# MLP of a decoder step: products of 448 columns for 224 tokens, 64 tokens as stationary tiles

## What is computed

```python
def hybrid_layer(x, cache_k, cache_v, h0_re, h0_im, p):
    ...
    h = x + mix @ p['w_out']
    y = h + jnp.square(jax.nn.relu(rmsnorm(h, p['mlp_norm_g']) @ p['w_mlp_up'])) @ p['w_mlp_down']
```

## Time and profile before

| | us |
|---|---|
| median of three runs | 1184.19 (1182.78 to 1184.59) |
| the profiled execution's own time | 1184.51 |
| its span, first to last instruction | 1182.7 |
| TensorE (PE) busy | 1174.5 |
| DVE, ACT, POOL busy | 749.6, 425.8, 139.2 |
| HBM read and written | 185.8 and 5.3 MB |

### The profile page before, as it was taken

One profiled execution on the slowest core, in us unless ns is written; L12 is line 12 of the kernel. 1 busy time (PEld: TensorE's weight loads), 2 busy tenths in 40 slices (PEclk: granted clock), 3 DMA queues, 4 the chain that ended last, 5 costly groups with the idle time before them and its releaser, 6 DMA issues.

```text
span 1182.7 us, 20247 instructions
## 1 busy us (share of the span) xinstructions
PE 1174.5 (99%) x8492; PEld 1104.5 (93%) x8492; DVE 749.6 (63%) x754; ACT 425.8 (36%) x515; POOL 139.2 (12%) x83
## 2 busy tenths in 40 slices
PE   9999999999999999999999999999999999999998
PEld 7577576799999999999999999999999999999998
DVE  7899899899776565544555554555564455565454
ACT  6100012975544333333333433333433333433331
POOL 0322512000000000100000110000110000110000
PEclk9899999999999999999999999999999999999999
DMA  7453333534445444454545455554445554445553
GB/s 290 137 140 125 111 115 126 175 122 143 162 157 191 170 161 167 154 178 165 174 161 166 155 178 165 171 164 163 158 152 188 170 168 160 161 148 184 174 171 117
DMA packets 55192, 190.29 MB, mean 161 GB/s; under 512 B 7864, under 2 KB 10168, under 8 KB 54712
## 3 DMA queue, kind: packets, MB, share of 16 engines
q1 hardware_dynamic: 54824, 188.79, 47.9%
q10 hardware_dynamic: 288, 0.30, 0.1%
HBM read 185.82 MB, written 5.28 MB: 162 GB/s over the span
## 4 chain that ended last, share of the span: by engine, by line
PE 94%; DVE 3%; issue 1%; ACT 1%; DMA 0%; SPq 0%
PE psum L1367 94%; DVE states L745 1%; DVE states L933 1%; DVE out_turn L745 0%; DVE turn L745 0%; DVE out_turn L975 0%; PE psum L1486 0%; DMA w_raw<-in_w 0%; ACT gate L606 0%; DVE q_t L993 0%; ACT L531 0%; DVE q_t L745 0%; ACT au L554 0%; DVE carry_p L745 0%; DVE kv_t L1025 0%
## 5 line engine op out<-in xcount | busy, mean ns | idle before, releaser
L736 DVE TENSOR_TENSOR w_lo<-w_raw,w_hi 128x1024 fp32r<-128x1024 f32 x292 | 407.1, 1406 | 385.5 <-ACT w_hi L450 384.7
L1367 PE MATMUL psum<-mov_b,w_hi 128*128 128x288 f32 x2624 | 522.4, 295 | 0.3 <-ACT gate L606 0.3
L450 ACT ACTIVATE w_hi<-w_raw 128x1024 fp32r<-128x1024 f32 x292 | 306.2, 1057 | 481.5 <-PE psum L1367 480.7
L1367 PEld LDWEIGHTS psum<-mov_b,w_hi 128*128 128x128 f32 x2624 | 419.8, 188 | 1.6 <-issue 0.7
L1367 PE MATMUL psum<-mov_a,w_hi 128*128 128x288 f32 x2048 | 406.6, 295 | 0.0
L1367 PE MATMUL psum<-mov_b,w_lo 128*128 128x288 f32 x1312 | 385.4, 294 | 0.0
L1367 PEld LDWEIGHTS psum<-mov_a,w_hi 128*128 128x128 f32 x2048 | 327.7, 188 | 0.1
L1367 PE MATMUL psum<-mov_a,w_lo 128*128 128x288 f32 x1024 | 300.7, 294 | 0.0
L1367 PEld LDWEIGHTS psum<-mov_b,w_lo 128*128 128x128 f32 x1312 | 247.6, 189 | 0.0
L1367 PEld LDWEIGHTS psum<-mov_a,w_lo 128*128 128x128 f32 x1024 | 193.3, 189 | 0.0
L1367 PE MATMUL psum<-x_g,w_raw 128*128 128x288 f32 x640 | 163.9, 414 | 0.3 <-DMA w_raw<-in_w 0.3
(11 more groups left out here) (182 smaller groups left out, 520.3 us busy)
## 6 DMA issues: line engine op xcount, KB each, us to landing
w_raw<-in_w SPq DMA_DIRECT2D x335, 512.0 KB, 3.3
h_t<-in_x SPq DMA_DIRECT2D x3, 576.0 KB, 8.4
out_y<-h_t SPq DMA_DIRECT2D x3, 576.0 KB
b_w<-in_b SPq DMA_DIRECT2D x1, 1024.0 KB, 7.5
c_w<-in_c SPq DMA_DIRECT2D x1, 1024.0 KB, 7.3
k_cache<-in_kc SPq DMA_DIRECT2D x1, 1024.0 KB, 5.8
v_cache<-in_vc SPq DMA_DIRECT2D x1, 1024.0 KB, 7.0
out_kc<-in_kc SPq DMA_DIRECT2D x1, 992.0 KB
```

Source lines behind the costliest of these rows:

```text
L450: nc.scalar.activation(hi3[:, n % SLOTS, :], raw3[:, n % SLOTS, :], ACT.Copy) \
L736: nc.vector.tensor_tensor(lo3[:, n % SLOTS, :], raw3[:, n % SLOTS, :], hi3[:, n % SLOTS, :].bitcast(F32), ALU.subtract) \
L1367: return nc.tensor.matmul(out, lhs_t, rhs, start=start, stop=stop)
```

## The change

**Tokens in two parts.** A is the first 224 tokens, B the last 64. A tile of tokens is now stored as low A, high A, high B, low B (224, 224, 64 and 64 columns). Per output tile and `k` there are two products with a stationary weight tile (`streams`): `w_hi` passes over low A and high A together, 448 columns, into 448 columns of the bank; `w_lo` over high A and high B, 288 columns, into columns 224 to 511. At `k` = 0 the first has 512 columns (high B with it), so that all of the bank is begun anew.

**B stationary.** The product of `w_hi` with B goes the other way round (`passing`): the 128 columns high B and low B are the stationary tile, and `w_hi` of all the unit's output tiles passes, 384 or 256 columns, into a fourth bank. Its rows are tokens and have to be turned: at `k` = 0 the stationary tile is `first_b`, zeros and low B.

**Units.** A row (up or down) has six units of 3, 3, 3, 3, 2 and 2 output tiles, each with one bank a tile and one for B. The steps of the first four have 768 columns (384 KB), those of the last two 1024 with four `k` of 256. A row has 40 steps in place of 32.

**Turning back.** In an up row, ACT copies the B bank as its high part `bres_hi`, DVE takes the rest `bres_lo`, and TensorE multiplies both with `stack` (two unit matrices of 64 on top of each other) in f32r, 64 columns, into columns 448 to 511 of the unit's banks (`turn_b`). This stands in TensorE's program behind `k` = 1 of the next unit. In a down row DVE adds the B bank to `b_sum` in SBUF, and only the last row turns the sums, in fp32. DVE then adds the two parts of A in the banks (`low_sum`).

**States in halves.** `turn_h0` takes half of the pairs; the first half stands ahead of `u_t`, the second ahead of the second half's states, and the carry factors stand behind `u_t`. The first DMAs on SP change places: the first weights, then `small`.

```diff
-BLOCK_STEPS = 8 * GROUP_STEPS
+TOK_B = 64
+TOK_A = TOK - TOK_B
+UNIT_OUTS = (3, 3, 3, 3, 2, 2)
+ROW_UNITS = len(UNIT_OUTS)
+UNIT_STEPS = (8, 8, 8, 8, 4, 4)
+FIRST_OUT = tuple(sum(UNIT_OUTS[:i]) for i in range(ROW_UNITS))
+FIRST_STEP = tuple(sum(UNIT_STEPS[:i]) for i in range(ROW_UNITS))
+ROW_STEPS = sum(UNIT_STEPS)
+ROWS = 8
+BLOCK_STEPS = 2 * ROW_STEPS
...
+        bres_hi, _ = sb("bres_hi", 3 * P, F32R, at=at_t1)
+        bres_lo, _ = sb("bres_lo", 3 * P, F32R, at=at_t1 + 4 * 3 * P)
+        stack_r, _ = sb("stack_r", TOK_B, F32R, at=at_t1 + 4 * 6 * P)
+        b_sum, _ = sb("b_sum", KT * P, at=at_bw)
+        b_first, _ = sb("b_first", 2 * P, F32R)
...
+        HI, LO_A, LO_B = slice(TOK_A, TOK_A + TOK), slice(0, TOK_A), slice(TOK_A + TOK, 2 * TOK)
+        first_b = b_first[:, :].rearrange("p (x c) -> p x c", x=2)
+        HI_A, HI_B = slice(TOK_A, 2 * TOK_A), slice(2 * TOK_A, TOK_A + TOK)
...
+            sp.dma_start(raw4[:, 0, 0, :], ins["w"][0, :, 0:STEP_N]).then_inc(w_first, 16)
             sp.dma_start(small[:, 0:first], ins["small"][:, 0:first]).then_inc(small_loaded, 16)
-            sp.dma_start(raw4[:, 0, 0, :], ins["w"][0, :, 0:STEP_N]).then_inc(w_first, 16)
...
+            def act_up(row, past=0):
+                for u in range(ROW_UNITS):
+                    hi_ahead(u, row, past, SLOTS + 1 - UNIT_STEPS[u], SLOTS - 1)
+                    bres_from(u, row, past)
+                    hi_ahead(u, row, past, SLOTS - 1, SLOTS + 1)
+                    hid_his(u, row, past)
...
+            one_over_root(UNIT["rms_x"], r_b)
+            turn_h0(0)
...
+            turn_h0(1)
...
+            def low_sum(part, u, row, past):
+                nc.vector.tensor_copy(part[:, :, 0:TOK_A], mlp_outs(u, slice(0, TOK_A))).then_inc(low_copied, 1)
+                dve.wait_ge(low_copied, (2 * past + row) * ROW_UNITS + u + 1)
+                tt(part[:, :, 0:TOK_A], part[:, :, 0:TOK_A], mlp_outs(u, slice(TOK_A, 2 * TOK_A)), ALU.add)
+            def up_out(u, row, past=0):
+                lo_ahead(u, row, past, SLOTS + 1 - UNIT_STEPS[u], SLOTS - 1)
+                dve.wait_ge(bres_out, past * ROW_UNITS + row // 2 * ROW_UNITS + u + 1)
+                cols = slice(0, UNIT_OUTS[u] * P)
+                tt(bres_lo[:, cols], mlp_b(u), bres_hi[:, cols].bitcast(F32), ALU.subtract).then_inc(bres_split, 1)
+                if u >= 2:
+                    dve.wait_ge(hid_lo, past * ROW_UNITS + row // 2 * ROW_UNITS + u - 1)
+                lo_ahead(u, row, past, SLOTS - 1, SLOTS + 1)
+                part = sr4[:, u % 2, 0:UNIT_OUTS[u], :]
+                dve.wait_ge(b_turned, past * ROW_UNITS + row // 2 * ROW_UNITS + u + 1)
+                low_sum(part, u, row, past)
+                nc.vector.tensor_copy(part[:, :, TOK_A:TOK], mlp_outs(u, slice(2 * TOK_A, 512))) \
+                    .then_inc(mlp_free[(N_UNITS + u) % 2], 1)
+                own_freed(row, u, past)
+                nc.vector.scalar_tensor_tensor(part, part, 0.0, part, ALU.max, ALU.mult).then_inc(hid_ready, 1)
...
+                summed = tt(b_sum[:, cols], b_sum[:, cols], mlp_b(u), ALU.add)
+                if last:
+                    summed.then_inc(b_summed, 1)
+                lo_ahead(u, row, past, SLOTS, SLOTS + 1)
+                if last:
+                    dve.wait_ge(b_turned, N_BLOCKS * ROW_UNITS + u + 1)
...
                 dve.wait_ge(last_full, o + 1)
-                link(tt(tb4[:, 1, o, :], banks(N_UNITS + 3)[:, o, :], r_b[:, :], ALU.mult))
-                linked()
-                tt(h3[:, 12 + o, :], h3[:, 12 + o, :], tb4[:, 1, o, :], ALU.add).then_inc(last_ready, 1)
+                part, out = tb4[:, 1, o, :], psum[:, mlp_bank(u) + o, :]
+                link(nc.vector.tensor_copy(part[:, 0:TOK_A], out[:, 0:TOK_A]))
+                linked()
+                link(tt(part[:, 0:TOK_A], part[:, 0:TOK_A], out[:, TOK_A:2 * TOK_A], ALU.add))
+                link(tt(part[:, TOK_A:TOK], out[:, 2 * TOK_A:512], r_b[:, TOK_A:TOK], ALU.mult))
+                linked()
+                link(tt(part[:, 0:TOK_A], part[:, 0:TOK_A], r_b[:, 0:TOK_A], ALU.mult))
+                linked()
+                tt(h3[:, 14 + o, :], h3[:, 14 + o, :], part, ALU.add).then_inc(last_ready, 1)
...
+            def hid_los(u, past=0, before=0):
+                pool.wait_ge(hid_hi, past * ROW_UNITS + before + u + 1)
+                part, tiles = sr4[:, u % 2, 0:UNIT_OUTS[u], :], xb3[:, FIRST_OUT[u]:FIRST_OUT[u] + UNIT_OUTS[u], :]
+                tt(tiles[:, :, LO_A], part[:, :, 0:TOK_A], tiles[:, :, HI_A].bitcast(F32), ALU.subtract)
+                if u == 0:
+                    tt(first_b[:, 1, TOK_B:P], part[:, 0, TOK_A:TOK], tiles[:, 0, HI_B].bitcast(F32), ALU.subtract)
+                tt(tiles[:, :, LO_B], part[:, :, TOK_A:TOK], tiles[:, :, HI_B].bitcast(F32), ALU.subtract) \
+                    .then_inc(hid_lo, 1)
...
+            def streams(u, o, k, w, tile, turned=False):
+                slot, at, out = w
+                w_h, w_l = (t[:, slot, at + o * P:at + (o + 1) * P] for t in (hi3, lo3))
+                cols = 512 if k == 0 else 2 * TOK_A
+                mm(out[:, o, 0:cols], w_h, tile[:, 0:cols], start=k == 0, stop=False)
+                return mm(out[:, o, TOK_A:512], w_l, tile[:, HI], start=False, stop=k == KT - 1 and not turned)
...
+            def passing(row, u, k, w, tile):
+                slot, at, _ = w
+                return mm(mlp_b(u), tile[:, 2 * TOK_A:2 * TOK] if k else first_b[:, row % 2, :], hi3[:, slot, at:at + UNIT_OUTS[u] * P],
+                          start=k == 0, stop=k == KT - 1)
+            def turn_b(u, row):
+                if row % 2 == 0:
+                    pe.wait_ge(bres_split, row // 2 * ROW_UNITS + u + 1)
+                    parts = ((bres_hi, stack_r), (bres_lo, stack_r))
+                else:
+                    pe.wait_ge(b_summed, u + 1)
+                    parts = ((b_sum[:, FIRST_OUT[u] * P:(FIRST_OUT[u] + UNIT_OUTS[u]) * P], stack),)
+                for o in range(UNIT_OUTS[u]):
+                    for i, (src, unit) in enumerate(parts):
+                        done = mm(mlp_outs(u, slice(2 * TOK_A, 512))[:, o, :], src[:, o * P:(o + 1) * P], unit[:, :],
+                                  start=False, stop=i == len(parts) - 1)
+                done.then_inc(b_turned, 1)
...
+            def mlp_unit(row, u, between=None):
+                mov, per = (xa3, xb3)[row % 2], KT // UNIT_STEPS[u]
+                set_free(row, u)
...
+                for k in range(KT):
+                    w, tile = slot_of(u, row, k), mov[:, k, :]
+                    if row == 0 and u == 0:
+                        pe.wait_ge(h_lo, k + 1)
+                    if row % 2 == 1 and u == 0 and k in FIRST_OUT:
+                        pe.wait_ge(hid_lo, row // 2 * ROW_UNITS + FIRST_OUT.index(k) + 1)
+                    for o in range(UNIT_OUTS[u]):
+                        streams(u, o, k, w, tile, turned=row % 2 == 0 or row == ROWS - 1)
+                    done = passing(row, u, k, w, tile)
+                    if k % per == per - 1:
+                        done.then_inc(step_used, 1)
+                    if k == 1 and between:
+                        turn_b(*between)
```

385 lines of the change are left out of this document (221 added, 164 removed).

## The result

The changed kernel takes 1213.57 us (median of four runs, 1212.56 to 1220.65) where the kernel before takes 1184.13 us (1182.78 to 1184.59): a ratio of 1.0272 with a 95% interval of 1.025 to 1.0293 (the medians alone give 1.025). It is slower by 29 us. One of its four runs, that of 1220.65 us, had a mean granted clock of 0.948 where the others had 0.997 to 0.999. The prediction had said 1168 us, within 1157 to 1206, and gave slower a chance of 0.31: it was wrong in the sign and in the range. Of its rivals R2, that the time goes by columns (1205 us), was nearest; the result lies above that one too.

What follows compares the result with a forecast made beforehand. TensorE was taken as the bound, busy for 99% of the span. From 1184.5 us, -16.1 (MLP), +3.5 (waits), +0.9 (end) and -5.2 (states in halves) sum to -16.9, giving 1168 us, range 1157 to 1206.

Steps and rivals of the forecast that it cites:

- R2: Rival for the MLP: time goes by columns at 2.18 a ns, fewer products bring nothing; 1205 us, chance 0.13.
- The 12.2 ns: MLP: a 288-column product's 132.2 ns less 120.0 of columns, read as uncovered load and hand-over; wider products pay only 2.5 ns.
- (a): Start: ten f32r warm-up products at half rate show nothing over their columns, no charge per product or per column.
- (b): Full fp32 products and 128-column turns through the identity, full clock: some 2.5 ns each over their columns.
- (c): Every product loads its own stationary tile: 0.82 ns a column or 105 ns for 128, beside a fixed part.
- Turns: MLP: products that turn B's results back, taken at 109 ns each: 17.5 us, from 7 to 21.
- R4: Rival: the new order does not keep up in 12 large units, 1 us each, +12: 1180 us, chance 0.07.
- Waits of the last row: Last row: TensorE waits for the turns, 3 x 0.2 + 1.5 + 1.3 us, +3.5 us.
- Weights, DVE, ACT, POOL: MLP: weight loads in 320 steps in place of 256 and DVE's additional instructions stay hidden, at no cost.
- End: Behind the last product: five DVE instructions in place of two, +0.9 us.
- States in halves: Before the first u_t: wait falls to about 0.5 us (-1.9), clock stays full (-3.3); together -5.2 us (0 to -5.7).
- The first two DMAs: Start: their new order moves the start by under half a us; nothing taken.

Runs made afterwards that it cites:

- experiment 1: Kernel before plus a strip of f32r products of 64 to 512 columns behind its end: 230.0 ns for 512 columns, 203.3 for 448, 133.2 for 288, 118.7 for 256.
- experiment 2: Kernel before with 5944 of the MLP's 6144 products cut in two halves of 144 columns, same columns in all: 1717.06 us.
- experiment 5: Kernel before plus a strip: 192 columns f32r with 128, 64, 32 stationary columns 111, 89, 87 ns; f32r and bf16 in turns of 1 135.0 ns, of 16 127.7.
- experiment 7: Kernel after with the small tensor again sent for ahead of the first weights: 1210.91 us.
- experiment 6: Kernel before with only the states in halves, the order of the first two DMAs left: 1181.05 us against 1182.41, ratio 0.9988.

## Why the prediction was wrong, step by step

**The bound** was read rightly: TensorE was it and stayed it.

**The 12.2 ns** is the step that failed. The prediction read them as what a load of 128 columns and a hand-over lack to be covered by 120 ns of columns, and concluded that a wider product costs its columns and 2.5 ns. A floor by the load exists (experiments 1, 2 and 5), but at 111 to 112 ns, below 133. What stands above the columns is a surcharge of f32r products that grows from 12 ns at 256 columns to 17 at 512, of which 3.4 ns at 288 columns go by the load. So 448 columns cost 206 in place of 189 ns, +33 us; the sign of being wrong that the prediction had named, over 195 ns, came true. The three rows were read too far: (a), nothing over the columns at half rate, excluded a charge at half rate and said nothing of full rate, as the text itself remarked under R2; (b), fp32 with 2.5 ns over, moves its bytes at half the rate; (c) gave 105 ns for a load, and the 27 ns to 132 were given to a hand-over that no row shows. The turns of (b), at 109 ns with loads of 128 columns, had already shown such a load through in less than 132, as the prediction said against itself. That the 256-column products would cost 132 ns was wrong with it: 118.

**R2** had the right side and nearly the seven-product time (1190). Its proportion is too simple, as experiment 1 shows, but its price for 448 columns (205.7 ns) is what the MLP showed. That is partly luck: the strip has 203.3, and a law by columns alone gives 118 at 256 and 235 at 512 for the 118.7 and 230.0 measured. It was given 0.13, though nothing but (b) spoke against it.

**Turns**: 17.5 us forecast, 16.2 measured, and nobody waited for them in the up rows. Right, and R4 was wrong. The f32r turns of 64 columns went at 111 ns, so the 109 that were taken from wider fp32 turns stood close to the floor.

**Waits of the last row**: +3.5 forecast. Measured are two places, before the two small units, in which the next product starts 1.58 and 2.14 us after the one before where 0.12 is usual, so 3.5 us in all. The split was off: 1.5 and 1.3 there and three times 0.2 before, of which nothing came. The clock was at its lower level for 3.4 us behind the second (about 1.7 us more), which was not forecast. Undoing both gave 4.5 to 5.3 us.

**Weights, DVE, ACT, POOL**: hidden, right (DMA share 0.52, DVE busy 515 of 842 us), but for one wait of 0.6 us for w_lo in the first up row, which the forecast had without waits.

**End**: +0.9 us forecast, 0.86 measured in DVE's instructions.

**States in halves**: the gap fell by 1.8 us and the clock stayed, as forecast, and yet the 1.9 us were not gained: the first group ended 2.3 us later, and TensorE resumed 0.5 us later than before. **The first two DMAs** were valued at nothing and cost some 1.9 us (experiment 7). The clock's fall was counted with 3.3 us as if it were in each run; it cost 2.5 us in the trace that the forecast was reckoned from, and of six traces with this front three have none there (experiment 6). Together the start brought 1.6 us at the MLP (265.48 in place of 267.12 us), not 5.2, and against the trace of before in which the clock never fell (264.46) it brought nothing.

The sum: the MLP took 42 us more than forecast and the start gained 3.6 us less, and 1168 becomes 1213.

## What to carry to other kernels

Before products are made wider to save a charge per product, measure one width that the kernel doesn't have yet: strips of 60 products behind its end tell charge, slope and floor apart in one run (here to within 3 or 4 ns of what the same product took in the kernel). Where products are bound by their columns, look at the type of the operands, not at the number of products, and keep products of one type together: 4096 bf16 products shortened the MLP by 3.6 us scattered and by 27.6 us in order. A second order of DMAs at the start deserves its own run, since it decided here when the first products start and how many of them run at the lower clock. And look at more than one trace before a fall of the clock is put into a sum: one trace shows it as if it were always there.

## What the runs showed that was not expected

- f32r at full clock costs 7.4 ns and 0.435 ns a column from 256 to 512 columns, bf16 its columns at 2.4 a ns and 2.5 ns; moving data at a distance of eight bytes cost two cycles a column in either type.
- The load of 128 stationary f32r columns is a floor of 111 to 112 ns, and of 213 ns at the lower clock; for bf16 56 ns a product was reached.
- Changing between f32r and bf16 costs some 14 ns for a pair of changes in turns of up to 4.
- The clock fell to its lower level in stretches in which TensorE was busy all the time: in products of 64 columns, and in four of six traces behind attention's products of 128 and 16 columns near 262 us; but not in 1333 us of products of 144 columns (experiment 2). Behind the gap ahead of u_t it fell in three of six traces, and not by the length of the gap alone (1.65 us did, 1.81 didn't).
- Open: why 448 and 384 columns cost 3 to 4 ns more in the MLP than in the strip, and what the last 3 ns are by which f32r is dearer than bf16 at the same distance.
